# A hybrid decoder layer on one core: split token loads, reordered tile steps, new PSUM banks and filler around the FFN start

## The chip, the core and the metric

The program runs on one core of one Trainium2 chip. The core has five engines with a queue each: TensorE (PE, matmuls and transposes into PSUM; its weight loads are shown as PEld), VectorE (DVE), ScalarE (ACT), GpSimd (POOL) and SyncE (SP), which here only issues DMA. The metric is the device time of one execution in microseconds (us), the median over runs.

## What is computed

One inference step of one layer, for 1024 prompt tokens and 8 x 4 = 32 decode tokens (N = 1056 columns), d_model 1024, all in float32:

```
h = rms_norm(x, ln_mix_pre)
qa, ka, va, qkvb, bb, ab, zb, qc, gates = split(h @ w_in)
oa = sliding window attention with sinks (qa, ka, va)
ob = gated delta rule over chunks (qkvb, bb, ab), then norm and silu(zb)
oc = attention of qc over 256 memory tokens
up = einsum('blnc,ncd->blnd', stack(oa, ob, oc), w_branch)
mix = sum(sigmoid(gates) * up) @ w_out
x = x + rms_norm(mix, ln_mix_post)
gt, uf = split(rms_norm(x, ln_ffn_pre) @ w_ffn_in)
x = x + rms_norm((silu(gt) * uf) @ w_ffn_out, ln_ffn_post)
```

## The kernel before

**Number format.** Every float32 product of the large matrices is made of three matmuls: both operands are split into a high part (hi, rounded) and a low part (lo, the rest), and hi x hi, hi x lo and lo x hi are added in PSUM. So a weight panel, once it has landed in `raw`, is split on POOL in two steps (L839 and L842, or L900 and L902 in `split_to`) into `wsp` or, for the output projection, into `wo_top`, `wo_mk`, `wo_br`, `wo_ac` and, for the last one, a half of `wsp`. Activations are split on ACT (hi) and DVE (lo).

**Tiling.** The 1056 columns are three chunks of CH = 352. A chunk of a panel is 8 blocks x 3 passes = 24 matmuls of 128 x 352 and one PSUM bank. `raw` and `wsp` have two slots; panel n uses slot n % 2, and `load` waits for the split of n - 2.

**Stages**, in order of time:
- Opening (to 60 us). Eleven token tiles: 0 to 7 of the prompt, 8 the decode tokens, 9 and 10 the memory. For each: ACT squares it (L1579), DVE makes the mean (L2013), ACT the root (L1584), DVE the reciprocal (L2015) and scales into `xs` (L2017); PE transposes it (L958); ACT copies the hi part (L1588) and DVE the lo part (L2023) into `actT`. ACT and DVE run these in a software pipeline, `tile_a(t)`: squares and norm of tile t + 1, hi and lo of tile t - 1. PE puts the six chunks of the first two panels (L994) between transposes. SP loads x in `load_pair`, tiles 2 and 3, 4 and 5, 6 and 7, and weights between them.
- Input projection, 27 panels (L970), to 394 us.
- Middle stage: eight tiles of 128 tokens, each a list of steps TILE that all engines walk through. Each tile holds the delta rule (decay `dec` and `decm`, `at`, the inverse in `xt` and `xx`), six score groups ("S", transposed in "T", applied in "V") and 144 gate matmuls (L1152) as filler.
- Decode stage: the 32 decode tokens, with the last eight gate panels as filler (`gate_mm`, L1232), 576 matmuls in all.
- Branch stage (1086 to 1240 us). 12 panels, three branches of four (r = j // 4). For panel j SP loads weights (`load_wb`) and the stored gates (`load_q`, tile `gat`); ACT makes the sigmoid (L1921); PE does six half chunks of 12 matmuls (L1458) into banks 0 to 2; DVE multiplies them with the gate and adds to `accT` (L2443, or L2448 and L2450). Branch inputs come by `load_br(r)` into `brw` (2.1 MB) and are split by `hi_br` on ACT (L1910) and `lo_br` on DVE (L2418). The mixed sum `accT` is split in the same way, `lo_mix(m)` for m = 0 to 3 whole (L2424), for m = 4 to 7 by chunk.
- Output projection: nine blocks of token rows, `out_rows(t)` (L1481, 48 matmuls of 128 x 512), each normed, added to x, normed again and transposed back (`turn_back`, L1492).
- FFN: 22 steps of a loop of gate panel, up panel (L1466) and output panel (L1524).

**Order around the change.** Each engine works through its queue in the order of the code, and waits for semaphores. `x_here(n)` lets SP wait for token tile n. `x_lo`, `x_nm` count lo parts and scaled tiles, `w_lo` split panels, `g_mm` finished chunks of PE, `g_ev` evacuated banks, `b_hi` and `b_lo` split branch and mix parts, `q_sg` sigmoids, `q_mx` mixed chunks, `f_st` finished stores of the decode stage, `u_lo` row blocks that are back in `actD`, `t_y` normed row blocks. UO is the count of chunks at the end of the branch stage.

## Time and profile before

| what | value |
|---|---|
| median of 3 runs | 2156.93 us (2152.8 to 2168.03) |
| the profiled execution | 2157.78 us, its span 2156.0 us |
| PE busy | 2084.3 us, 97% |
| DVE / ACT / POOL busy | 46% / 24% / 35% |
| mean granted clock of PE | 0.986 |
| DMA | 193.80 MB, 90 GB/s over the span |
| chain that ended last | PE 85%, DVE 7%, ACT 4%, DMA 2%, issue 2% |

How to read it: the span is covered by PE nearly throughout, so the idle time of other engines costs nothing by itself; what counts is where PE stands still, and who releases it then. The granted clock is the share of full speed (2.4 GHz) that PE had; 0.50 is its lower level, 1.2 GHz.

### The profile page before, as it was taken

What the parts mean: (1) busy time and instruction counts of PE and PEld (TensorE: products, weight loads), DVE (VectorE), ACT (ScalarE), POOL (GpSimd) and SP (SyncE); (2) the same over time, 40 slices, a digit from 0 to 9 for tenths busy, and PEclk for the clock granted to TensorE, in tenths of its full rate; (3) what the DMA queues carried; (4) which work ended last, traced back from release to release, by engine and by line L of the source; (5) the groups of instructions that cost most, each with busy time, mean ns of one, the idle gap of its engine ahead of it and who ended that gap; (6) DMA issues with size and microseconds to landing.
All of it is one profiled execution on the core that took longest, in us unless ns stands there. A gap on an engine that the chain in (4) does not pass through costs nothing.

```text
span 2156.0 us, 34339 instructions
## 1 busy us (share of the span) xinstructions
PE 2084.3 (97%) x13511; PEld 2017.7 (94%) x13511; DVE 995.4 (46%) x1667; ACT 515.7 (24%) x1137; POOL 761.0 (35%) x325
## 2 busy tenths in 40 slices
PE   6999999999999999999999979999999999999998
PEld 5999999999999999999889968899999999999997
DVE  5754620355555555411347944533434353434435
ACT  5333621333333333321032222200000000000002
POOL 3334873111110111122136531343443434443444
PEclk8999999999999999999999999999999999999999
DMA  5223333433222332164375432111111111111114
GB/s 179 90 79 101 109 99 104 131 100 100 64 72 75 92 100 65 43 179 123 99 238 183 157 117 81 61 40 48 49 39 48 49 39 49 39 49 48 49 39 172
DMA packets 221271, 193.80 MB, mean 90 GB/s; under 512 B 24715, under 2 KB 192267, under 8 KB 221154
## 3 DMA queue, kind: packets, MB, share of 16 engines
q1 hardware_dynamic: 207042, 182.72, 27.5%
q10 hardware_dynamic: 14128, 9.65, 1.4%
q8 instruction: 73, 1.20, 0.2%
q14 instruction: 28, 0.23, 0.0%
HBM read 146.26 MB, written 47.09 MB: 90 GB/s over the span
## 4 chain that ended last, share of the span: by engine, by line
PE 85%; DVE 7%; ACT 4%; DMA 2%; issue 2%; SPq 0%; ACTq 0%; DVEq 0%
PE psum L1466 23%; PE psum L970 13%; PE psum L1524 11%; PE psum L1080 7%; PE psum L1152 6%; PE psum L1481 5%; PE psum L1232 4%; PE psum L1458 3%; PE psum L1201 2%; ACT pr L1795 1%; PE psum L1190 1%; DMA brw<-s_br 1%; PE psum L1035 1%; PE psum L1174 1%; PE psum L994 1%
## 5 line engine op out<-in xcount | busy, mean ns | idle before, releaser
L839 POOL TENSOR_TENSOR wsp<-raw,kc 128x1024 fp32r<-128x1024 f32 x116 | 277.6, 2393 | 1179.6 <-PE psum L1152 434.0
L1466 PE MATMUL psum<-actD,wsp 128*128 128x352 f32 x3168 | 517.2, 323 | 0.9 <-DVE actD L2482 0.9
L1466 PEld LDWEIGHTS psum<-actD,wsp 128*128 128x128 f32 x3168 | 511.3, 189 | 1.1 <-DVE actD L2482 1.1
L842 POOL TENSOR_TENSOR wsp<-raw,wsp 128x1024 fp32r<-128x1024 f32 x116 | 288.4, 2486 | 9.1
L970 PE MATMUL psum<-actT,wsp 128*128 128x352 f32 (+1 forms) x1728 | 282.5, 324 | 0.0
L970 PEld LDWEIGHTS psum<-actT,wsp 128*128 128x128 f32 (+1 forms) x1728 | 272.7, 185 | 5.4
L2535 DVE TENSOR_TENSOR accT<-accT,psum 128x352 f32<-128x352 f32 x504 | 241.7, 520 | 50.1 <-PE psum L1524 50.1
L1524 PE MATMUL psum<-fT,wsp 128*128 128x352 f32 x1512 | 249.8, 323 | 0.4 <-DVE accT L2535 0.4
L1524 PEld LDWEIGHTS psum<-fT,wsp 128*128 128x128 f32 x1512 | 244.0, 188 | 0.7 <-DVE accT L2535 0.7
L1152 PE MATMUL psum<-actT,wsp 128*128 128x352 f32 x1152 | 216.4, 333 | 0.0
L2518 DVE TENSOR_TENSOR fr<-psum,sg 128x352 f32<-128x352 f32 x66 | 34.6, 524 | 380.7 <-PE psum L1466 379.3
L1152 PEld LDWEIGHTS psum<-actT,wsp 128*128 128x128 f32 x1152 | 184.2, 188 | 0.8
L1458 PE MATMUL psum<-actD,wsp 128*128 128x352 f32 x864 | 144.7, 329 | 9.1 <-DVE prd L2448 4.6
L1458 PEld LDWEIGHTS psum<-actD,wsp 128*128 128x128 f32 x864 | 142.4, 193 | 11.4 <-DVE prd L2448 6.3
L1977 ACT ACTIVATE sg<-psum 128x352 f32<-128x352 f32 x66 | 30.5, 464 | 433.8 <-PE psum L1466 433.8
L1232 PE MATMUL psum<-actT,wsp 128*128 128x352 f32 x576 | 110.2, 344 | 0.0
L1232 PEld LDWEIGHTS psum<-actT,wsp 128*128 128x128 f32 x576 | 97.8, 200 | 4.8 <-issue 4.5
L1985 ACT ACTIVATE fT<-fr 128x352 fp32r<-128x352 f32 x66 | 32.9, 498 | 237.2 <-DVE fr L2518 237.2
L1795 ACT ACTIVATE pr<-psum,asm 128x256 f32<-128x256 f32 x96 | 44.6, 469 | 125.6 <-DVE asm L2228 73.1
L2140 DVE TENSOR_TENSOR kd<-psum,par 128x512 f32<-128x512 f32 x8 | 5.5, 691 | 119.6 <-PE psum L1089 119.6
L2055 DVE TENSOR_SCALAR y<-cv,scT 128x1024 f32<-128x1024 f32 (+1 forms) x24 | 32.3, 1385 | 58.3 <-ACT y L1655 54.5
L2058 DVE SCALAR_TENSOR_TENSOR y<-cv,scT,y 128x1024 f32<-128x1024 f32 x72 | 58.1, 854 | 0.9 <-DVE y L2058 0.4
(426 smaller groups left out, 2600.0 us busy)
## 6 DMA issues: line engine op xcount, KB each, us to landing
raw<-in_w_in SPq DMA_DIRECT2D x100, 256.0 KB, 4.0
raw<-in_w_ffn_in SPq DMA_DIRECT2D x88, 256.0 KB, 3.2
gat<-s_gate SPq DMA_DIRECT2D x12, 1056.0 KB, 5.3
raw<-in_w_ffn_out SPq DMA_DIRECT2D x44, 256.0 KB, 2.8
s_gate<-gst SPq DMA_DIRECT2D x48, 176.0 KB, 1.8
s_qkv<-y SPq DMA_DIRECT2D x12, 528.0 KB, 3.0
brw<-s_br SPq DMA_DIRECT2D x3, 2112.0 KB, 9.9
raw<-in_w_branch SPq DMA_DIRECT2D x24, 256.0 KB, 5.2
```

The lines of the kernel that those rows point to most:

```text
L839: pool.tensor_tensor(wsp[:, slot, 0], raw[:, slot], ones.unsqueeze(1).to_broadcast([P, KT, P]), ALU.mult).then_inc(w_hi, 1)
L842: pool.tensor_tensor(wsp[:, slot, 1], raw[:, slot], wsp[:, slot, 0].bitcast(F32), ALU.subtract).then_inc(w_lo, 1)
L970: mm = pe.matmul(psum[0:m, c, 0:CH], wsp[:, slot, a, k, 0:m], actT[:, h, k, CH * c:CH * c + CH], start=(k == 0 and q == 0), stop=(k == KT ...
L1080: mm = pe.matmul(psum[:, bank, w * h:w * h + w], lhs(h), rhs(h), start=True, stop=True)
L1152: mm = pe.matmul(psum[:, c, 0:CH], wsp[:, (NPB + j) % 2, a, kt, :], actT[:, h, kt, CH * c:CH * c + CH], start=(n % 24 == 0), stop=(n % 24 ...
L1232: mm = pe.matmul(psum[:, c, 0:CH], wsp[:, (NPB + m) % 2, a, k, :], actT[:, h, k, CH * c:CH * c + CH], start=(y % 24 == 0), stop=(y % 24 == ...
L1458: mm = pe.matmul(psum[:, c, 0:CH], slab(wsp[:, :, a], slot)[:, k, P * half:P * half + P], actD[:, h, a4 + k, CH * c:CH * c + CH], start=(k ...
L1466: mm = pe.matmul(psum[:, bank, 0:CH], wsp[:, slot, a, k, :], actD[:, h, k, CH * c:CH * c + CH], start=(k == 0 and q == 0), stop=(k == KT - ...
L1481: mm = pe.matmul(psum[0:rows, 2 * slot + half, :], actD[:, h, (k + 4) % 8, P * t:P * t + rows], wo_part(k, a)[:, 512 * half:512 * half + 512],
L1524: mm = pe.matmul(psum[:, 4 + x % 4, 0:CH], wsp[:, slot, a, m, :], fT[:, fs, h, CH * c:CH * c + CH], start=(q == 0), stop=(q == 2))
L1795: mm = act.activation(pr[:, a, :], psum[:, 3, 256 * a:256 * a + 256], ACT.Exp, scale=A_SC[j], bias=asm[:, S_NM, 2 * j + a:2 * j + a + 1], ...
L2535: dve.tensor_tensor(accT[:, m, cols], accT[:, m, cols], psum[:, 4 + x % 4, 0:CH], ALU.add).then_inc(o_ad, 1)
```

## The change

It has six parts.

1. **Opening.** Token tiles 2 and 3 are loaded one by one, each followed by a weight panel, and the pairs (4, 5) and (6, 7) wait for tiles 2 and 3. On DVE the mean of tile t + 1 stands ahead of the lo part of tile t - 1.
2. **Middle stage.** On DVE the multiplication `decm` moves from its own step to the head of step "KK", behind the score maximum and its two small steps of group 0.
3. **Decode stage.** The filler of gate matmuls is dealt out anew: 78 instead of 72 first, 18 instead of 12 ahead of the memory scores, 17 instead of 18 ahead of each of eight, 10 instead of 14 ahead of `update(7)`. The sum stays 576.
4. **Branch stage.** `load_br(1)` is issued ahead of the weights and gates of panel 2, `load_br(2)` at j == 3 instead of 4. The sigmoid of panel 2 stands ahead of the hi parts of branch 1. The hi and lo parts of mix 0 to 3 come half a panel to a panel sooner.
5. **Output projection.** The row blocks use banks 3 to 6 instead of 0 to 3 and the transposes back banks 0 and 1 instead of 4 and 5; PE's wait for g_ev ahead of them is gone; the split of the last projection weights on POOL also waits for the lo parts of the first chunk.
6. **FFN start.** Chunks 0 and 1 of the up panel (NPF + 1) are done between and behind the last two transposes back, ahead of chunk 2 of the gate panel, in banks 5 and 6. The third panel (NPF + 2) is split on POOL after five chunks instead of three, since it overwrites the gate panel.

```
-    X_LAND = ((0, 16), (1, 16), (0, 32), (0, 32), (1, 32), (1, 32), (0, 48), (0, 48), (1, 48), (0, 64), (0, 64))
+    X_LAND = ((0, 16), (1, 16), (0, 32), (1, 32), (0, 48), (0, 48), (1, 48), (1, 48), (0, 64), (1, 64), (1, 64))
...
         x_here(0)
-        load_pair(2)
+        sp.dma_start(xin[:, 2, :], x_view[2]).then_inc(x_in[0], 16)
         load_b(0)
         x_here(1)
-        load_pair(4)
+        sp.dma_start(xin[:, 3, :], x_view[3]).then_inc(x_in[1], 16)
         load_b(1)
         x_here(2)
+        load_pair(4)
+        x_here(3)
         load_pair(6)
...
         sp.wait_ge(f_st, F_ST)
+        load_br(1)
         for c in range(3):
             sp.wait_ge(gs_st[c], 16 + 16 * 24)
         for j in range(12):
             if j + 2 < 12:
                 load_seq(W_N["b", j + 1] - NPD + 1, W_N["b", j + 2] - NPD + 1)
                 load_q(j + 2)
-            if j in (0, 4):
-                load_br(j // 4 + 1)
+            if j == 3:
+                load_br(2)
...
                 if j == 7:
                     pool.wait_ge(g_mm, 6 + UO)
+                    pool.wait_ge(b_lo, 1 + MIX_N(0, 7) + 1)
...
-                    done = (3, 6, 9)[j]
+                    done = (5, 6, 9)[j]
...
-        gate_mm(72)
+        gate_mm(78)
         pe.wait_ge(f_in, F_IN)
...
-        gate_mm(12)
+        gate_mm(18)
         pe.wait_ge(f_dv, DVn("el"))
...
-            gate_mm(18)
+            gate_mm(17)
             mem_scores(b)
...
-        gate_mm(14)
+        gate_mm(10)
         update(7)
...
-                        mm = pe.matmul(psum[0:rows, 2 * slot + half, :], actD[:, h, (k + 4) % 8, P * t:P * t + rows],
+                        mm = pe.matmul(psum[0:rows, 3 + 2 * slot + half, :], actD[:, h, (k + 4) % 8, P * t:P * t + rows],
...
-
-        pe.wait_ge(g_ev, 3 + UO)
...
-                mm = pe.transpose(psum[:, 4 + k // 4, P * (k % 4):P * (k % 4) + rows],
+                mm = pe.transpose(psum[:, k // 4, P * (k % 4):P * (k % 4) + rows],
...
-            full_chunk(NPF % 2, c, 6 + c)
+            full_chunk(NPF % 2, c, (7, 2)[c])
         turn_back(NT - 1, 1, P)
+        pe.wait_ge(w_lo, NPF + 1 + 3)
+        pe.wait_ge(t_y, 2 + NT)
+        full_chunk((NPF + 1) % 2, 0, 5)
         turn_back(NT, 0, NS)
+        pe.wait_ge(u_lo, 2 + 6)
+        full_chunk((NPF + 1) % 2, 1, 6)
...
-        full_chunk(NPF % 2, 2)
-        in_panel(NPF + 1, (NPF + 1) % 2, g_ev, 3 + UF)
+        full_chunk(NPF % 2, 2, 3)
+        in_panel(NPF + 1, (NPF + 1) % 2, g_ev, 3 + UF, chunks=(2,))
...
+        def sigmoid(j):
+            act.wait_ge(q_in[j % 2], 16 * (j // 2) + 16)
+            act.activation(gat[:, j % 2], gat[:, j % 2], ACT.Sigmoid).then_inc(q_sg, 1)
+
         for j in range(12):
+            if j == 2:
+                sigmoid(j)
             for half in range(2):
                 if (j, half) in BR_AT:
                     hi_br(*BR_AT[j, half])
-            if j == 11:
-                for m in range(4):
+            if j >= 10:
+                for m in (2 * (j - 10), 2 * (j - 10) + 1):
...
+            if first:
+                mean(t + 1, 1 - b, first)
             if last:
                 lo_x(t - 1, 1 - b, last[0], last[1], last[2] if last[1] is memT else P * t - P)
...
-                elif step == "DEC":
+                elif step == "KK":
                     dve.wait_ge(dec_ok, 2 * t + 2)
                     dve.wait_ge(mrk_ok, t + 1)
                     dve.wait_ge(kq_ok, t + 1)
                     dve.tensor_tensor(decm[:], dec[:], mrk[:], ALU.mult).then_inc(dm_ok, 1)
-                elif step == "KK":
...
-                if j >= 10:
-                    lo_mix(2 * (j - 10) + half)
+                if 2 * j + half >= 19 and 2 * j + half < 23:
+                    lo_mix(2 * j + half - 19)
```

The rest of the diff gives ACT and DVE the new bank numbers.

What the change does to the order of instructions is shown at three places. First DVE, at the start of the first tile of the middle stage. L2147 (L2164 in the change) is `decm`; `asm` holds the score maximum and what follows from it. Before:

```order
118 L2140 TENSOR_TENSOR kd<-psum,par 128x512
119 L2142 TENSOR_TENSOR vb<-psum,par 128x512
120 L2147 TENSOR_TENSOR decm<-dec,mrk 128x512
121 L2220 TENSOR_REDUCE asm<-psum 128x2
122 L2223 SCALAR_TENSOR_TENSOR asm<-asm,snk 128x2
123 L2226 TENSOR_TENSOR asm<-asm,snk 128x2
124 L2152 TENSOR_TENSOR at<-psum,decm 128x512
```

With the change:

```order
118 L2157 TENSOR_TENSOR kd<-psum,par 128x512
119 L2159 TENSOR_TENSOR vb<-psum,par 128x512
120 L2236 TENSOR_REDUCE asm<-psum 128x2
121 L2239 SCALAR_TENSOR_TENSOR asm<-asm,snk 128x2
122 L2242 TENSOR_TENSOR asm<-asm,snk 128x2
123 L2164 TENSOR_TENSOR decm<-dec,mrk 128x512
124 L2168 TENSOR_TENSOR at<-psum,decm 128x512
```

`decm` has moved behind the three steps of the scores, next to `at`, which reads it; the same holds in all eight tiles.

Second SP's queue at the start of the branch stage; `s_br` is the stored branch input, `s_gate` the stored gates. Before:

```order
236 L723 DMA s_br<-dob 128x4x32
237 L649 DMA raw<-in_w_branch 64x4x256 x2
238 L672 DMA gat<-s_gate 128x2x1056
239 L667 DMA brw<-s_br 128x4x1056
240 L649 DMA raw<-in_w_branch 64x4x256 x2
241 L672 DMA gat<-s_gate 128x2x1056
```

With the change:

```order
236 L725 DMA s_br<-dob 128x4x32
237 L669 DMA brw<-s_br 128x4x1056
238 L651 DMA raw<-in_w_branch 64x4x256 x2
239 L674 DMA gat<-s_gate 128x2x1056
240 L651 DMA raw<-in_w_branch 64x4x256 x2
241 L674 DMA gat<-s_gate 128x2x1056
```

The load of `brw` has moved ahead of the weights (row 238) and the gates (row 239) of panel 2.

Third PE around the last two transposes back (L1492, L1494 in the change); L1466 (L1470) are the chunks of the first FFN panels. Before:

```order
827 L1492 MATMUL psum<-kc,xs 128x128 x8
828 L1466 MATMUL psum<-actD,wsp 128x352 x48
829 L1492 MATMUL psum<-kc,xs 128x128 x8
830 L1492 MATMUL psum<-kc,xs 128x32 x8
831 L1466 MATMUL psum<-actD,wsp 128x352 x120
```

With the change:

```order
827 L1494 MATMUL psum<-kc,xs 128x128 x8
828 L1470 MATMUL psum<-actD,wsp 128x352 x48
829 L1494 MATMUL psum<-kc,xs 128x128 x8
830 L1470 MATMUL psum<-actD,wsp 128x352 x24
831 L1494 MATMUL psum<-kc,xs 128x32 x8
832 L1470 MATMUL psum<-actD,wsp 128x352 x96
```

One chunk of 24 matmuls now stands between the two transposes; the number of chunks is the same.

## Rows read from the trace of the kernel before

**Rows 1.** TensorE's waits over the whole span: total us, times, longest

```profile
PE psum L958 <- DVE xs L2017: 20.1, 6, 9.2
...
PE psum L1190 <- ACT pr L1795: 12.5, 16, 1.5
...
PE psum L1458 <- DVE prd L2448: 4.6, 5, 2.9
...
PE psum L1247 <- DMA da<-s_qc: 2.0, 1, 2.0
...
PE psum L1291 <- DVE del_ L2302: 1.6, 1, 1.6
```

**Rows 2.** Chain of work (start, us), then a window (busy, granted clock, DMA share)

```profile
1429.72 19.24 PE psum L1466 x120
...
1250.00:1254.00 4.00, 2.83 (x7) 2.25 (x8) 3.38 (x8) 1.13 (x3) 0.00 (x0) 0.50 0.19 76
```

**Rows 3.** Timeline of the opening: start us, us, engine, line [idle before <-releaser]

```profile
8.19 1.06 ACT L1579 ACTIVATE xjunk<-xin 128x1024 f32<-128x1024 f32 x1 [0.61 <-DMA xin<-in_x_prompt]
...
12.09 0.78 SPq L477 DMA_DIRECT2D xin<-in_x_prompt  x1
...
19.44 3.42 DVE L2017 SCALAR_TENSOR_TENSOR xs<-xin,rs,gbc 128x1024 f32<-128x1024 f32 x1
...
27.84 5.04 PE L994 MATMUL psum<-actT,wsp 128*128 128x352 f32 x24
...
28.02 1.28 DVE L2017 SCALAR_TENSOR_TENSOR xs<-xin,rs,gbc 128x1024 f32<-128x1024 f32 x1
...
31.53 1.28 DVE L2017 SCALAR_TENSOR_TENSOR xs<-xin,rs,gbc 128x1024 f32<-128x1024 f32 x1
...
45.35 1.09 PE L958 MATMUL psum<-kc,xs 128*128 128x128 f32 x8 [1.53 <-DVE xs L2017]
```

**Rows 4.** Timeline of the first steps of tile 1 of the middle stage

```profile
460.64 2.38 POOL L842 TENSOR_TENSOR wsp<-raw,wsp 128x1024 fp32r<-128x1024 f32 x1
...
461.74 1.82 DVE L2147 TENSOR_TENSOR decm<-dec,mrk 128x512 f32<-128x512 f32 x1 [1.93 <-ACT dec L1769]
...
463.49 0.68 DVE L2220 TENSOR_REDUCE asm<-psum 128x2 f32<-128x512 f32 x1
...
464.50 0.69 DVE L2152 TENSOR_TENSOR at<-psum,decm 128x512 f32<-128x512 f32 x1
...
465.47 0.66 PE L1190 MATMUL psum<-kc,pr 128*128 128x128 f32 x4 [1.54 <-ACT pr L1795]
```

**Rows 5.** DMA issues of 1100.27, 1100.69 and 1101.20 (KB each, us to landing)

```profile
gat<-s_gate SPq DMA_DIRECT2D x1, 1056.0 KB, 7.2
...
brw<-s_br SPq DMA_DIRECT2D x1, 2112.0 KB, 14.1
...
raw<-in_w_branch SPq DMA_DIRECT2D x2, 256.0 KB, 13.8
```

**Rows 6.** Timeline at panel 2 of the branch stage

```profile
1116.78 1.95 ACT L1921 ACTIVATE gat<-gat 128x2112 f32<-128x2112 f32 x1
...
1120.98 48.01 PE L1458 MATMUL psum<-actD,wsp 128*128 128x352 f32 x288 [3.97 <-DVEq L2445]
```

**Rows 7.** Timeline between branch stage and output projection

```profile
1240.13 7.82 DVE L2424 TENSOR_TENSOR actD<-accT,actD 128x352 fp32r<-128x352 f32 x4
...
1244.63 2.50 POOL L902 TENSOR_TENSOR wsp<-raw,wsp 128x1024 fp32r<-128x1024 f32 x1
...
1248.86 1.82 DVE L2424 TENSOR_TENSOR actD<-accT,actD 128x352 fp32r<-128x352 f32 x4
...
1251.17 4.93 PE L1481 MATMUL psum<-wo_top,actD 128*128 128x512 f32 x12 [10.92 <-DVE prd L2448]
```

**Rows 8.** Timeline of TensorE at the start of the FFN

```profile
1371.45 1.03 PE L1492 MATMUL psum<-kc,xs 32*128 32x32 f32 x8 [3.19 <-DVE actD L2482]
...
1373.41 40.88 PE L1466 MATMUL psum<-actD,wsp 128*128 128x352 f32 x240 [0.93 <-DVE actD L2482]
```

More of the change, by code:

```diff
@@ L1985, in hi_f @@
                 act.activation(fT[:, fs, 0, CH * c:CH * c + CH], fr[:, CH * c:CH * c + CH], ACT.Copy).then_inc(f_hi, 1)
-        gt_panel(0, 0, banks=(6, 7, 2))
+        gt_panel(0, 0, banks=(7, 2, 3), order=(1, 2, 5))
         hi_f(0, 0)
@@ L1997, in _ @@
             act.wait_ge(t_tr, 9 + t + 1)
[L1998 removed]
+            act.activation(jk[0:rows, :], rows_psum(2 * slot, rows), ACT.Square,
                            accum_out=ns[0:rows, slot % 2, slot // 2, 0:1]).then_inc(t_sq, 1)
@@ L2008, in _, with mean, norm @@
         dve.wait_ge(k_in, 16 * 2)
-        def norm(n, slot, rows, gain):
+        def mean(n, slot, rows):
             dve.wait_ge(x_sq, n + 1)
             dve.tensor_scalar(rs[0:rows, slot, 1:2], rs[0:rows, slot, 0:1], 1.0 / D, EPS, ALU.mult, ALU.add).then_inc(x_rs, 1)
+        def norm(n, slot, rows, gain):
             dve.wait_ge(x_rt, n + 1)
@@ L2239, in dve_tile @@
                         level(2)
-                elif step[0] == "D":
+                elif step[0] == "D" and step != "DEC":
                     f = step[1]
@@ L2508, in _, with mul_f @@
         dve.memset(accT[:], 0.0).then_inc(o_ad, 1)
-        def mul_f(i):
-            for c in range(3):
+        def mul_f(i, banks=(0, 1, 2)):
+            for c, bank in enumerate(banks):
                 cols = slice(CH * c, CH * c + CH)
@@ L2542, in step_f @@
             add_out(i - 1, range(4, KT))
-        mul_f(0)
+        mul_f(0, banks=(5, 6, 2))
         lo_f(0, 0)
```

33 lines of the change are left out of this document (16 added, 17 removed).

## The prediction

> **What bounds the kernel.** The profile's first part comes first: TensorE (PE) is busy for 97% of the span, so only three things can shorten the run: PE's idle time, PE's time at half clock, and less work on it. The diff removes no matmul. So the next view is PE's waits: 20.1 + 12.5 + 4.6 + 2.0 + 1.6 [rows 1], and in the timelines 4.0 [rows 6], 10.9 [rows 7] and 3.2 + 0.9 [rows 8], 59.8 us together. A warm chunk (24 matmuls) takes 19.24 / 5 = 3.85 us, a matmul 0.16 [rows 2]. The window at the end of the wait of 10.9 has a granted clock of 0.50 [rows 2]: PE works at 1.2 instead of 2.4 GHz, so a removed wait returns the slow time behind it too. The sum is made against the profiled execution, 2157.8 us (span 2156.0 and 1.8 around it); the median of the runs shown, 2156.9, needs no correction.
>
> **Opening.** PE's first chunk follows the transposes of tile 4 and starts at 27.84; ahead of it DVE scales a tile every 3.51 us (L2017 at 28.02 and 31.53) [rows 3]. In this cycle stand mean, ACT's root and reciprocal between the low part and the scaling. With the mean ahead, mean and root run under the low part: some 0.5 less a tile. The pair of tiles 2 and 3 held the queue from tile 1's landing at 8.19 to 12.09 [rows 3], so tile 2 alone lands 2.0 earlier. Part of this is eaten again: tiles 4 and 5 are asked for only then, behind three transfers, and POOL's weight splits still hold one scaling (L2017 took 3.42 instead of 1.28) [rows 3]. I take 3.1 for the first chunk and 1.4 of the wait of 1.53 for tile 9 [rows 3]: **4.5**, bounds 2.5 (only the shorter cycle, 5 x 0.5) and 6.5 (2.0 for the load, 2.5 for the cycle, 2.1 for the hold).
>
> **Tiles.** In each of the eight tiles of the middle stage DVE now takes the score maximum (L2220) ahead of decm (L2147). PE waits for the exponentials that follow, 1.54 in this tile [rows 4]; of 12.5 us in 16 waits [rows 1] seven are of this kind. The maximum could start 3 us before 463.49: decm began at 461.74, when ACT had the decay, and took 1.82 us where such an operation takes 0.69 (L2152), ending 0.54 after POOL's split step (460.64 to 463.02) [rows 4]. So POOL holds a DVE operation with two SBUF operands. The maximum reads PSUM and passes, but its next step (L2223: asm and snk, both SBUF) is held to 463.02; before, it came at 463.49 + 0.71 = 464.20. That is 1.2. `at` follows decm, which ends some 0.4 later than 463.56; but `at` stood behind the maximum before, so it starts at 464.1 instead of 464.50, and with PE 1.2 ahead the inverse's transposes may wait 0.2. Seven by 1.0: **7.0**, bounds 3 (the inverse waits 0.8) and 10.8 (7 x 1.54, no hold).
>
> The Trainium skill (SBUF — State Buffer, Who interferes with whom) calls this an exclusive lock: a DVE instruction with two SBUF inputs and a GpSimd instruction that reads SBUF block each other fully, and a tensor_reduce is never held. By it a tile gains 1.2, without it 1.54; the trace's 1.82 agrees with the lock.
>
> **Decode stage.** Six gate matmuls more stand ahead of the wait for f_in (2.0) and six ahead of that for `el` (1.6) [rows 1]; each six fills 6 x 0.16 = 0.96. They come from fillers ahead of eight score steps (one each) and of an update (four), where PE has no wait now: **1.9**, bounds 0 (it waits there instead) and 2.5 (with clock).
>
> **Branch stage, panel 2.** Its gates were issued at 1100.27 and landed 7.2 later, at 1107.5 [rows 5], but their sigmoid began at 1116.78 [rows 6]: two ACT copies of brw stood ahead, and brw landed at 1100.69 + 14.1 = 1114.8 [rows 5]. PE waited 4.0 [rows 6] and, by the clock of rows 2, some 3.4 us of half clock cost 1.7 more. Now the sigmoid goes first. The load also goes 2.4 earlier, ahead of panel 2's weights, and transfers land in order of issue: weights behind brw took 13.8 [rows 5]. brw's 2.1 MB needed 7.3 (1107.5 to 1114.8), so it lands near 1106, the weights near 1108.5, and their split, two POOL steps of 2.4 [rows 4], ends at 1113.3. PE wants them at 1120.98 - 4.0 - 5.8 (three chunks of 12 matmuls into free banks) = 1111.2 [rows 6]. A new wait of 2.1 takes the place of 5.7: **3.6**, bounds 1.5 and 5.7.
>
> The Trainium skill (DMA: Bandwidth & Descriptors, Queues, rings and completion order) says that each DMA engine takes descriptors in ring order, which speaks against this early load: by it the term is 3.6, by free sharing of the queue up to 5.7. The 13.8 agrees with the order.
>
> **Panel 6** is the same once more: the load moves one panel ahead; 2.9 of the waits for prd [rows 1] is here, with 1.7 of slow clock. DVE has little slack after it: **3.5**, bounds 1 and 5.
>
> **Ahead of the output projection** PE stops for 10.92 us [rows 7]. It waited for the last evacuation, which stood in DVE's queue behind four low parts (L2424). These took 7.82 instead of 1.82 (the same four at 1248.86) while POOL split the last projection weights [rows 7]. That wait of PE is gone, since the rows use banks 3 to 6, and this split waits for the low parts. Low parts 0 to 3 come half a panel sooner, so the first row block can run k = 0 to 3 at once: 24 matmuls of 0.16 x 512 / 352 = 0.23, 5.6 us, while the others need 1.8. The split then runs from about 1240.5 to 1245.4 and is wanted at k = 7, 42 x 0.23 = 9.8 after 1240.25. Behind it on POOL wait the first FFN split and the residual adds; the first add is wanted only by a transposition two row blocks (22 us) later. The slow start, 4.93 instead of 12 x 0.23 = 2.8 [rows 7], goes too: **13.0**, bounds 10 and 13.5.
>
> **FFN start.** PE waits 3.19 and 0.93, and its next chunk takes 40.88 - 9 x 3.85 = 6.2 instead of 3.85 [rows 8, 2]: 6.4 us. Two chunks of the second panel now fill this. But the third panel's weights may be split only after five chunks instead of three, and the split (4.8) has one chunk (3.85) as cover: 1.0 of new wait. **5.4**, bounds 4 and 6.4.
>
> Sum: 4.5 + 7.0 + 1.9 + 3.6 + 3.5 + 13.0 + 5.4 = 38.9; 2157.8 - 38.9 = **2118.9 us**. The lower bounds add up to 22.0 (2135.8), the upper ones to 50.4 (2107.4).
>
> **Rivals.**
> - The stop moves into the output projection: low parts 4 to 7 are held by POOL's earlier splits (7.8 instead of 1.8), or the norm gains and residual rows, which SP can send only when DVE has finished, come late. For it: DVE is a chunk behind when PE ends. Against: 5.6 us of ready work. It costs 7.8 - 5.6 = 2.2 with slow clock behind it and, in the row loads, up to 5: 2125. Chance 0.12.
> - The early 2.1 MB loads starve weights and gates, so both branch terms vanish. For it: 13.8 behind brw. Against: the second load has a whole panel of slack. 2118.9 + 7.1 = 2126. Chance 0.12.
> - The tile reorder does not do what it says, because POOL holds the maximum's next step as long as the old order did; 7.0 becomes 1, 2125. It needs a hold to 464.2, past the step's end at 463.02. Chance 0.08.
> - Slower: decm now stands behind three steps that need scores, so behind awin and qz from DMA. If those are late, the decay chain at, xt, inverse stalls in all eight tiles. It decides once that chain is (38.9 - 7.0) / 8 = 4.0 us a tile later than PE can use it; at 7 us the time is 2157.8 - 31.9 + 56 = 2182. Against: the loads are issued a tile ahead, and PE's waits have no row for them. Chance 0.03.
> - As summed, 2110 to 2130: 0.60. The last 0.05 is several of these at once, up to no change.
>
> **The numbers.** A measurement here tells 1%, 21.6 us, from no change. The forecast and its first three rivals each pass that; the mixed case (0.05) and a share of 0.03 of the rivals with low bounds elsewhere do not. So faster 0.89, same 0.08, slower 0.03. The range runs from the upper bounds, 2107, to just past the lower ones, 2137.
>
> **What would show it.** First L994 chunk at 24 to 25 us; waits of PE for pr of a few tenths; panel 2's sigmoid at the landing of its gates, with a wait of PE of about 2 for weights; no wait and a granted clock of 1.0 between the last branch chunk and the first projection rows; 1 us of wait for the third FFN split. The forecast is wrong if PE stops within the projection rows, if L1190 waits as before, or if a step of the FFN loop changes, which the sum takes as untouched.

## The result and the profile after

| what | before | after |
|---|---|---|
| median | 2158.8 us (4 runs) | 2123.9 us (4 runs: 2119.8 to 2134.7) |
| ratio after / before | | 0.9836, 95% interval 0.9804 to 0.9868 |
| profiled execution; span | 2157.8; 2156.0 us | 2124.25; 2122.4 us |
| PE busy; granted clock | 97%; 0.986 | 98%; 0.993 |

The change makes the kernel 1.6% faster; the interval of the ratio lies wholly below 1, from 1.3 to 2.0%. It is 34.9 us between the medians and 33.6 between the spans; forecast were 38.9. The profile after, first PE's waits over the whole span (total us, times, longest):

```profile
PE psum L962 <- DVE xs L2032: 16.1, 5, 9.2
PE psum L1462 <- DVE prd L2464: 5.8, 3, 2.9
PE psum L1194 <- ACT pr L1802: 2.9, 15, 0.2
PE psum L1462 <- DVE actD L2416: 1.8, 1, 1.8
PE psum L1251 <- DMA da<-s_qc: 1.2, 1, 1.2
...
PE psum L1295 <- DVE del_ L2318: 0.6, 1, 0.6
PE psum L1470 <- POOL wsp L845: 0.3, 1, 0.3
```

The waits for `pr` fell from 12.5 to 2.9, those of 10.9 ahead of the output projection and 3.2 at the FFN start are gone [rows 1, 7, 8]. But in the branch stage (L1462, L1458 before) PE still waits 5.8 + 1.8 us, in part at places where it hardly waited before. The timeline of PE through this stage and into the projection rows (L1485) shows where (start us, us, engine, line, [idle before <- releaser]):

```profile
1070.76 3.96 PE L1462 MATMUL psum<-actD,wsp 128*128 128x352 f32 x15
1076.52 22.51 PE L1462 MATMUL psum<-actD,wsp 128*128 128x352 f32 x129 [1.79 <-DVE actD L2416]
1099.18 52.40 PE L1462 MATMUL psum<-actD,wsp 128*128 128x352 f32 x324 [0.15 <-POOL wsp L905]
1153.98 13.54 PE L1462 MATMUL psum<-actD,wsp 128*128 128x352 f32 x72 [2.41 <-DVE prd L2464]
1168.00 34.90 PE L1462 MATMUL psum<-actD,wsp 128*128 128x352 f32 x216 [0.47 <-DVE prd L2464]
1205.83 19.14 PE L1462 MATMUL psum<-actD,wsp 128*128 128x352 f32 x108 [2.94 <-DVE prd L2464]
1224.81 2.95 PE L1485 MATMUL psum<-wo_top,actD 128*128 128x512 f32 x12
```

A panel is 72 matmuls. So PE stops in panel 0 (1.79; before, 0.53), not at panel 2 (0.15 instead of 3.97), in panel 6 (2.41, as before), and in panel 10 (2.94; before, waits of 0.2 to 0.4). The stage took 153.8 us, before 153.5: it gained nothing. This is no accident of the two executions: from its first to its last matmul it took 153.5 to 156.1 us in the profiles of the four kernels with the old branch stage (before and, in the experiments, b_tiles, b_mean and b_load), and 153.8, 153.7 and 156.7 in the three with the new one (after, a_gev, a_nopw).

The time between the first matmuls of two stages, in both profiled executions, tells what each part brought:

| stretch | before | after | gain | forecast |
|---|---|---|---|---|
| opening, to the first matmul of the third panel | 59.7 | 56.5 | 3.2 | 4.5 |
| input projection | 338.5 | 337.0 | 1.5 | 0 |
| middle stage (tiles) | 513.2 | 504.5 | 8.7 | 7.0 |
| decode stage | 175.0 | 172.8 | 2.2 | 1.9 |
| branch stage, first to last matmul | 153.5 | 153.8 | -0.3 | 7.1 |
| gap ahead of the projection + projection | 11.3 + 108.2 | 0.2 + 106.3 | 13.0 | 13.0 |
| FFN start, to the first output panel | 54.7 | 49.4 | 5.3 | 5.4 |
| the rest | 741.9 | 741.9 | 0 | 0 |

So the sum's error of 5.3 us is the branch stage's 7.4, in part covered by other terms; 1.5 of this cover, the input projection, is luck.

### The profile page after: what moved, and what is told of

It is laid out like the page before. It is cut to its first block, busy times and chain, and to the rows that moved or that the text cites. A ratio compares the mean times of both kernels' runs of the same rounds, so it can differ in the third digit from the quotient of the medians.

```text
span 2122.4 us, 34341 instructions
## 1 busy us (share of the span) xinstructions
PE 2081.3 (98%) x13511; PEld 2014.4 (95%) x13511; DVE 1003.6 (47%) x1667; ACT 515.5 (24%) x1137; POOL 758.0 (36%) x325
## 4 chain that ended last, share of the span: by engine, by line
PE 89%; DVE 5%; DMA 2%; ACT 1%; issue 1%; SPq 1%; POOL 0%; DVEq 0%; POOLq 0%; ACTq 0%
PE psum L1470 24%; PE psum L974 13%; PE psum L1531 11%; PE psum L1084 7%; PE psum L1156 6%; PE psum L1485 5%; PE psum L1462 4%; PE psum L1236 4%; PE psum L1205 2%; PE psum L1178 1%; PE psum L998 1%; PE psum L1194 1%; ACT pr L1802 1%; PE psum L1039 1%; PE psum L1573 1%
## 5 line engine op out<-in xcount | busy, mean ns | idle before, releaser
L1470 PE MATMUL psum<-actD,wsp 128*128 128x352 f32 x3168 | 515.8, 323 | 1.0 <-ACT sg L1990 0.6
L1470 PEld LDWEIGHTS psum<-actD,wsp 128*128 128x128 f32 x3168 | 509.1, 188 | 1.6 <-issue 0.9
L1462 PE MATMUL psum<-actD,wsp 128*128 128x352 f32 x864 | 146.4, 332 | 7.8 <-DVE prd L2464 5.8
L1462 PEld LDWEIGHTS psum<-actD,wsp 128*128 128x128 f32 x864 | 144.2, 195 | 10.0 <-DVE prd L2464 7.1
```

Of the source, the lines that this page charges most:

```text
L1462: mm = pe.matmul(psum[:, c, 0:CH], slab(wsp[:, :, a], slot)[:, k, P * half:P * half + P], actD[:, h, a4 + k, CH * c:CH * c + CH], start=(k ...
L1470: mm = pe.matmul(psum[:, bank, 0:CH], wsp[:, slot, a, k, :], actD[:, h, k, CH * c:CH * c + CH], start=(k == 0 and q == 0), stop=(k == KT - ...
```

## Experiments

Each kernel is compared with the kernel before on the same chip; stretches are read from its profiled execution. "Panels 0 to 2, 3 to 8, 9 to 11" are PE's waits in these parts of the branch stage; where two numbers stand, the first is panel 0 and the second the stop in panel 2.

| kernel | ratio, 95% interval | panels 0-2 | 3-8 | 9-11 |
|---|---|---|---|---|
| before | 1 | 0.53 + 3.97 | 3.75 | 0.84 |
| after | 0.9836 (0.9804 to 0.9868) | 1.79 + 0.15 | 2.88 | 2.94 |
| a_nopw | 0.9845 (0.9803 to 0.9887) | 0.67 + 3.70 | 3.58 | 4.13 |
| a_brold | 0.9871 (0.9834 to 0.9907) | 0.63 + 2.63 | 3.87 | 3.28 |
| a_br2mid | 0.9818 (0.9779 to 0.9856) | 0 | 1.19 | 4.14 |
| a_lo | 0.9813 (0.9782 to 0.9845) | 0 | 3.61 | 3.14 |
| a_p1 | 0.9822 (0.9791 to 0.9853) | 2.76 + 1.78 | 2.89 | 2.96 |
| a_gev | one execution | 0.66 + 3.00 | 3.62 | 3.28 |
| a_o3 | 0.9828 (0.9781 to 0.9876) | 0.62 + 4.28 | 3.80 | 3.11 |
| a_both | 0.9852 (0.9811 to 0.9893) | 3.07 + 1.97 | 1.68 | 3.05 |
| a_w2 | 0.9816 (0.9783 to 0.9849) | 3.12 + 0 | 1.19 | 3.62 |

### The opening: each half alone

Edits to the kernel before, each with one execution (2169.07 and 2157.93 us; the kernel before beside them had a median of 2162.1, from 2152.0 to 2169.1), so that only the trace tells something. First the loads (with the loads of tiles 3 to 7 and the landing counts as in the change):

```
-        load_pair(2)
+        sp.dma_start(xin[:, 2, :], x_view[2]).then_inc(x_in[0], 16)
...
```

> The kernel before with one part of the opening alone: tiles 2 and 3 loaded one by one, mean where it was. In the changed kernel the first full chunk began 2.25 us sooner (25.59 for 27.84), where 3.1 had been forecast. Theory 'landings': what comes first is set by when tiles 2, 4 and 5 land, and the load split gives nearly all: first chunk 1.5 to 2.3 us sooner than in the kernel before (25.5 to 26.3). Theory 'cycle' (the forecast's: 0.5 us a tile from the mean): the load gives at most 0.5 at the first chunk (27.3 or later), since DVE's cycle of 3.5 us a tile and POOL's hold eat it. In both, DVE scales a tile every 3.5 us in the steady part.

And the mean:

```
+            if first:
+                mean(t + 1, 1 - b, first)
             if last:
                 lo_x(t - 1, ...
```

> The kernel before with the other part of the opening alone: mean of the next tile ahead of the low part, loads as they were. Theory 'landings': first chunk at most 1.0 us sooner (26.8 or later), the steady cycle 3.15 us instead of 3.51, as in the changed kernel, so the gain comes only over the tiles behind the fifth. Theory 'cycle': first chunk 1.5 to 2.5 us sooner (25.3 to 26.3), 0.5 us a tile.

Timeline of b_load, then of b_mean: the first full chunk.

```profile
21.71 3.27 DVE L2019 SCALAR_TENSOR_TENSOR xs<-xin,rs,gbc 128x1024 f32<-128x1024 f32 x1
...
26.65 5.79 PE L996 MATMUL psum<-actT,wsp 128*128 128x352 f32 x24
```

```profile
22.07 2.00 DVE L2019 SCALAR_TENSOR_TENSOR xs<-xin,rs,gbc 128x1024 f32<-128x1024 f32 x1
...
25.75 5.99 PE L994 MATMUL psum<-actT,wsp 128*128 128x352 f32 x24
```

The loads alone gave 1.2 us at the first chunk and 0.4 at the end of the opening; the mean alone 2.1 and 2.8; both 2.2 and 3.2 in the changed kernel's profile. So "landings" falls, although the loads' 1.2 lies between what the two theories gave them. The second half of "cycle" holds in its size (the mean carries most), its 0.5 us a tile does not: DVE's steady cycle went from 3.51 us to 3.15 in the changed kernel and 3.31 in b_mean. The two kernels also differ in how long POOL held DVE's scaling just before the first chunk (the rows above, 3.27 against 2.00 us), so up to 1.3 us of the difference between them may be this hold and not the edits. This hold is not the same in every execution. In two kernels whose opening is the same, first a_gev:

```profile
21.27 1.28 DVE L2034 SCALAR_TENSOR_TENSOR xs<-xin,rs,gbc 128x1024 f32<-128x1024 f32 x1
21.46 3.33 POOL L845 TENSOR_TENSOR wsp<-raw,wsp 128x1024 fp32r<-128x1024 f32 x1
```

then a_nopw:

```profile
20.83 2.34 POOL L845 TENSOR_TENSOR wsp<-raw,wsp 128x1024 fp32r<-128x1024 f32 x1
20.90 3.35 DVE L2031 SCALAR_TENSOR_TENSOR xs<-xin,rs,gbc 128x1024 f32<-128x1024 f32 x1
```

Who comes first, by 0.07 or 0.19 us, takes its normal time and the other gets 1.0 to 2.1 us longer. Of the ten executions with this opening (after and nine kernels below) four (a_p1, a_lo, a_br2mid, a_gev) never had a scaling held to over 3 us like this, and their first chunk began at 23.3 to 24.2; the six others began at 25.5 to 26.1. The opening ended 4.6 to 6.5 us sooner than before in the four and 2.5 to 3.7 in the six. The Trainium skill (SBUF — State Buffer, SBUF: two separate sides) says that whichever of the two starts first gets the port pair for its whole instruction; the rows agree.

### The tiles alone

On the kernel before, the three lines of `decm` moved from step "DEC" to the head of step "KK".

> The kernel before with the reordered DVE steps of the middle stage's tiles alone. In the changed kernel this stage was 8.7 us shorter. Theory: the order does all of it: the stage shorter by 8 to 9.5 us, PE's waits for the exponentials 0.2 each, ratio 0.9955 to 0.9965. Rival: part of the 8.7 comes from the different phase in which the stage is entered (loads and POOL's splits stand otherwise against PE after the opening's 4.7): then 5 to 7 us here, ratio 0.997 to 0.998. Second rival (from the forecast): what the stage gains, the decode stage behind it loses, because the branch input it must load stays where it was: then total below 5 us.

Ratio 0.9953, interval 0.9932 to 0.9973; the middle stage is 8.7 us shorter, and PE's waits for `pr` fell as in the changed kernel. This stretch was 8.5 to 8.8 us shorter in every kernel with the new order. The first theory holds: the order does all of it, independent of the phase in which the stage is entered. Tile 1 in the profile after:

```profile
454.97 0.69 DVE L2236 TENSOR_REDUCE asm<-psum 128x2 f32<-128x512 f32 x1 [0.45 <-PE psum L1178]
455.35 2.38 POOL L845 TENSOR_TENSOR wsp<-raw,wsp 128x1024 fp32r<-128x1024 f32 x1
455.69 2.05 DVE L2239 SCALAR_TENSOR_TENSOR asm<-asm,snk 128x2 f32<-128x2 f32 x1
457.89 0.69 DVE L2164 TENSOR_TENSOR decm<-dec,mrk 128x512 f32<-128x512 f32 x1
...
458.86 0.66 PE L1194 MATMUL psum<-kc,pr 128*128 128x128 f32 x4 [0.21 <-ACT pr L1802]
```

The maximum passes beside POOL, its next step, on two columns only, is held to 457.74, the end of POOL's step (455.35 + 2.38 = 457.73), and still PE waits 0.21 instead of 1.54 [rows 4]. In the rows 4 `decm` was itself held to 1.82; now it takes 0.69, since the hold has been served by the small step.

### The output projection

Two single edits of the changed kernel. One takes POOL's new wait away, one puts PE's old wait back.

```
-                    pool.wait_ge(b_lo, 1 + MIX_N(0, 7) + 1)
```

> The changed kernel without POOL's new wait for the low parts of the first chunk ahead of the split of the last projection weights. Theory 'banks' (the rows' own banks 3 to 6 carry the gain at the output projection): POOL may start this split when the last branch matmul ends, at 1224.6, and in the changed kernel it started at 1225.34, so only 0.7 us is at stake: first projection rows begin at once after the last branch matmul as before, span within 1 us of the changed kernel, ratio to the kernel before 0.983 to 0.985. Theory 'POOL hold' (the forecast's: the split would hold low parts 4 to 7, 7.8 us instead of 1.8): PE stops 2 to 5 us in the projection rows, ratio 0.985 to 0.9875.

```
+        pe.wait_ge(g_ev, 3 + UO)
```

> The changed kernel with PE's old wait ahead of the projection rows put back: it waits for the last evacuation of the branch stage although its rows now have their own banks. Theory 'banks' (what is worth 11.1 us between the last branch matmul and the rows, and 1.9 behind it, is that PE no longer waits here): in the changed kernel DVE ended that evacuation near 1232.0, 7.4 us behind the last branch matmul, so PE waits 7 to 8 here, plus 1 to 2 of half clock behind it: gap plus projection 8 to 10 us longer than in the changed kernel. Theory 'POOL hold gone' (POOL's later split alone had already made the evacuations quick): wait below 3.

Without POOL's wait: gap and projection 13.0 us shorter than before, as with it. With PE's wait (timeline of PE in a_gev):

```profile
1219.39 2.19 PE L1462 MATMUL psum<-actD,wsp 128*128 128x352 f32 x12 [0.48 <-DVE prd L2466]
1229.42 5.49 PE L1485 MATMUL psum<-wo_top,actD 128*128 128x512 f32 x12 [7.84 <-DVE prd L2466]
```

It waits 7.84, the next 12 matmuls take 5.49 instead of 2.95, and gap and projection are 10.5 us longer than in the changed kernel. So the banks carry 10.5 of the 13.0; the other 2.5, by which this kernel is still shorter than the kernel before, is not taken apart by any run. The wait on POOL is worth nothing: in the profile after, POOL's split began 0.37 us behind the end of the last branch matmul (1205.83 + 19.14 = 1224.97), in a_nopw 0.08. There it holds the first chunk's four low parts (3.52 us), in the changed kernel, with the wait, the second chunk's:

```profile
1225.34 1.89 POOL L903 TENSOR_TENSOR wsp<-raw,kc 128x1024 fp32r<-128x1024 f32 x1 [4.25 <-PE psum L1462]
...
1227.54 4.03 DVE L2440 TENSOR_TENSOR actD<-accT,actD 128x352 fp32r<-128x352 f32 x4
```

### The branch stage, undone and shifted

a_brold: both loads of `brw` and the sigmoid as in the kernel before.

```
-        load_br(1)
...
-            if j == 3:
-                load_br(2)
+            if j in (0, 4):
+                load_br(j // 4 + 1)
...
-            if j == 2:
-                sigmoid(j)
...
```

> The changed kernel with the branch part undone: both later loads of brw and the sigmoid's place as in the kernel before. The forecast gave this part 3.6 (panel 2) + 3.5 (panel 6); the profiles of before and after give 5.2 and 0.7. Theory 'by term': PE's wait at panel 2 comes back (3 to 4.5 us, for the sigmoid), panel 6 keeps a wait of 2 to 3 of about the size the changed kernel has (2.41), and the branch stage is 3 to 6 us longer than the changed kernel's 153.8 (some 158), ratio to the kernel before 0.985 to 0.9875. Rival 'no net gain': the wait for POOL's split of panel 2's weights, which a second execution of this order shows at 3.70 us, costs as much as the wait for the gates did: branch stage within 1.5 us of the changed kernel's, ratio 0.983 to 0.985.

PE waited 2.63 for the gates at panel 2, 2.99 and 0.88 for `prd` in panels 6 and 7. The branch stage took 157.3 us, 3.5 more than in the changed kernel: "by term" is what the waits at panel 2 and 6 say. But it is only 0.6 more than in a_nopw (156.7), whose branch loads are the new ones and whose PE waited 3.70 us for the split weights at panel 2, as the rival has it. The ratios' intervals overlap too. What the branch part is worth as a whole is not shown; it lies within what executions differ by.

a_br2mid: only the second load moves, behind the weights of panel 6.

```
+                if j == 4:
+                    load_br(2)
                 load_q(j + 2)
-            if j == 3:
-                load_br(2)
```

> The changed kernel with the second of the two early loads put one weight pair later: brw for panels 8 to 11 is asked for after the weights of panel 6 instead of ahead of the second output-projection weights, still ahead of the gates of panel 6. Theory 'pile-up' (the wait of 2.41 at panel 6 stays because the projection weights land late behind brw, at 1136.1, and four pairs of POOL's splits then run back to back from 1136.1 to 1155.7 and hold each of DVE's additions): here POOL's splits start near 1131 with pauses between them, the additions in panel 5 are held half as often, and PE's wait in panel 6 falls to 0 to 1.2. Rival 'low parts': DVE is late there because four low parts of 1.25 to 3 us stand in two panels, wherever POOL's splits are: the wait stays at 2 to 3. Rival 'landing': brw now lands late and its copies hold the gates' sigmoid: wait of 1.5 to 4 for ACT or gates. Ratio to the kernel before 0.982 to 0.984 by the first, 0.983 to 0.986 by the others.

POOL in panels 5 and 6, first in the profile after:

```profile
1136.14 1.89 POOL L903 TENSOR_TENSOR wo_top<-raw,kc 128x1024 fp32r<-128x1024 f32 x1 [8.86 <-DMA raw<-in_w_out]
1138.11 2.57 POOL L905 TENSOR_TENSOR wo_top<-raw,wo_top 128x1024 fp32r<-128x1024 f32 x1
1140.63 2.18 POOL L903 TENSOR_TENSOR wsp<-raw,kc 128x1024 fp32r<-128x1024 f32 x1
...
1152.46 3.28 POOL L905 TENSOR_TENSOR wsp<-raw,wsp 128x1024 fp32r<-128x1024 f32 x1
```

and DVE beside it, an addition with both operands in SBUF that takes 0.53 when POOL rests:

```profile
1134.67 0.53 DVE L2466 TENSOR_TENSOR accT<-accT,prd 128x352 f32<-128x352 f32 x1
...
1138.88 2.18 DVE L2466 TENSOR_TENSOR accT<-accT,prd 128x352 f32<-128x352 f32 x1
```

In a_br2mid the same splits start at 1128.39 and pause after the second pair:

```profile
1128.39 2.02 POOL L903 TENSOR_TENSOR wo_top<-raw,kc 128x1024 fp32r<-128x1024 f32 x1 [2.11 <-DMA raw<-in_w_out]
...
1142.27 1.90 POOL L903 TENSOR_TENSOR wo_mk<-raw,kc 128x1024 fp32r<-128x1024 f32 x1 [4.44 <-DMA raw<-in_w_out]
```

and PE runs from panel 0 into panel 6 without a stop (480 matmuls):

```profile
1073.94 78.80 PE L1462 MATMUL psum<-actD,wsp 128*128 128x352 f32 x480
1153.16 9.89 PE L1462 MATMUL psum<-actD,wsp 128*128 128x352 f32 x60 [0.43 <-DVE prd L2464]
```

PE's waits in panel 6 were together 2.41 to 2.85 us in all six executions with this load as in the changed kernel (after, a_nopw, a_lo, a_p1, a_gev, a_o3), the longest 2.40 to 2.43, and 0.43, 0.67 and 0.42 in the three with it moved (a_br2mid, a_both, a_w2). "Pile-up" is shown. The branch stage took 147.6 us in a_br2mid, 6.2 less than in the changed kernel; 1.7 of this is less waiting in panels 3 to 8, most of the rest comes from panels 0 to 2, which ran without a stop (see "How much is chance").

a_lo: low and high parts 0 to 3 of the sum back at their old places.

> The changed kernel with the low parts 0 to 3 of the branch sum (and ACT's high parts) put back to their old places, half a panel later. In the changed kernel PE waits 2.94 at 1205.83, in panel 10, where the kernel before waited 0.2 to 0.4. Theory 'moved low parts': the wait comes from the low parts, now in panels 9 and 10 between two back-to-back splits of POOL: here the waits of panels 9 to 11 are together below 1.2, the branch stage 2.5 to 5 us shorter, and the output projection is at most 1 us longer, because the first row block needs low part 3 only 7.4 us after it starts; ratio 0.9815 to 0.9835. Rival 'POOL alone': DVE's additions are held by the splits there wherever the low parts stand, waits of 2 to 4 remain in panels 9 to 11, and the ratio is that of the changed kernel, 0.9836. Rival 'the stop moves': PE waits 2 to 5 in the first row block for low part 3 or 4.

PE waits 3.14 in panel 10, no less than in the changed kernel (2.94). So the moved low parts are not needed for it. In this kernel POOL splits four pairs from 1190.20 to 1209.1 without a pause; in the changed kernel it pauses 1.9 us between the second and third of them, and a low part of 3.42 stands behind. The kernels of the opening bear this out. b_load has the whole old branch stage, low parts included, and in it POOL splits the four pairs from 1213.59 to 1232.49 without a pause. PE then waits as in a_lo (rows of POOL, DVE and PE):

```profile
1222.88 2.19 POOL L902 TENSOR_TENSOR wo_br<-raw,kc 128x1024 fp32r<-128x1024 f32 x1
...
1230.19 3.42 DVE L2426 TENSOR_TENSOR actD<-accT,actD 128x1056 fp32r<-128x1056 f32 x1
...
1234.10 19.11 PE L1460 MATMUL psum<-actD,wsp 128*128 128x352 f32 x108 [2.79 <-DVE prd L2450]
```

In before, b_mean and b_tiles, with the low parts at the old place and a pause of 2.1 to 2.2 us between the second pair and the third, the waits of panels 9 to 11 are 0.8 to 0.9 together. In after and a_brold, with a pause of 1.9 to 2.0 and the low parts moved, they are 2.94 and 3.28. By these seven executions either is enough, splits without a pause or the moved low parts: DVE has no reserve there. No run changes the pause alone.

a_o3: the fourth pair of projection weights ahead of panel 9's.

```
-             ("b", 8), ("b", 9), ("o", 3), ("b", 10)
+             ("b", 8), ("o", 3), ("b", 9), ("b", 10)
```

> The changed kernel with one entry of the order of weights moved: the fourth pair of output-projection weights is loaded and split ahead of the branch weights of panel 9 instead of behind them. In panels 9 and 10 of the changed kernel POOL splits four pairs (4 x 4.6 = 18.5 us in 21.1) and PE waits 2.94 there; it waited 3.14 with the low parts at their old place, 3.28 with the old loads. Theory 'POOL share': with three pairs there and the fourth in panel 8, where POOL stood idle 7.7 us, DVE catches up: waits in panels 9 to 11 together 0 to 1.3, branch stage 2.5 to 5 us shorter than in the changed kernel; ratio to the kernel before 0.981 to 0.983. Rival 'DVE alone': DVE has 6.6 us of evacuations and a low part or two in each 11.5, so the wait only moves to panel 8 or stays: waits of 2 to 4 in panels 7 to 11, ratio 0.983 to 0.985.

The wait moved from panel 10 to panel 11 (2.66 at 1212.77) and kept its size. "POOL share" falls, the rival stands: what is late next takes the place.

### The entry of the branch stage

a_p1: POOL splits panel 1's weights only behind the second chunk's low parts.

```
+                if j == 1:
+                    pool.wait_ge(b_lo, 1 + 8)
```

> The changed kernel with one wait more on POOL: the split of the weights of panel 1 begins only when DVE has the second chunk's four low parts. In the changed kernel this split (1071.6 to 1076.1) held those four to 5.18 us instead of 1.83, and PE waited 1.79 for them, with half the clock around it. Theory 'hold': the low parts take 1.8, PE's wait at the second chunk is 0 to 0.3, the split ends by 1079 and panel 1 begins without a wait; branch stage 2 to 4 us shorter than the changed kernel's 153.8, ratio 0.982 to 0.9835. Rival: PE is simply early and the stop moves to panel 2 (wait for the split of its weights, 2 to 4), which is set by the loads behind the last decode store and not by PE: branch stage as before, ratio 0.9836.

In the profile after POOL's split holds these four low parts to 5.18 (the first four took 1.83):

```profile
1071.58 1.89 POOL L903 TENSOR_TENSOR wsp<-raw,kc 128x1024 fp32r<-128x1024 f32 x1 [6.40 <-DMA raw<-in_w_branch]
...
1072.15 5.18 DVE L2416 TENSOR_TENSOR actD<-brw,actD 128x352 fp32r<-128x352 f32 x4 [0.63 <-ACT actD L1911]
```

In a_p1 these four are free of the hold, and the third chunk's four get it:

```profile
1072.46 1.83 DVE L2418 TENSOR_TENSOR actD<-brw,actD 128x352 fp32r<-128x352 f32 x4 [0.60 <-ACT actD L1913]
1074.42 1.90 POOL L903 TENSOR_TENSOR wsp<-raw,kc 128x1024 fp32r<-128x1024 f32 x1 [6.32 <-DVE actD L2418]
1074.93 5.24 DVE L2418 TENSOR_TENSOR actD<-brw,actD 128x352 fp32r<-128x352 f32 x4 [0.44 <-ACT actD L1913]
```

PE waited 0.97 and 1.79 for low parts in panel 0 and 1.78 at panel 2. So the cause is right (1.83 for 5.18), but the stop only moved on, and the stage was 1.4 us longer than in the changed kernel: as a remedy the theory falls, to the rival's side.

a_both (a_br2mid and a_o3 together) and a_w2 (a_br2mid, and panel 2's weights asked for ahead of the stores):

> The changed kernel with both: brw's second load behind the weights of panel 6, and the fourth projection weights ahead of panel 9's. Theory: the two remedies add, since they act on panels 5 and 6 and on 9 and 10: from panel 3 to the last branch matmul PE waits less than 1.5 us together (5.8 in the changed kernel, 4.9 with the load alone), the branch stage is 147 to 149 us long, and the ratio to the kernel before is 0.978 to 0.9815, below the changed kernel's 0.9836. Rival: the chip's clock in the decode stage, which made that stage 8 to 11 us longer in three of nine executions, and the waits for brw and panel 2's weights, which come when PE is early, take it back: ratio 0.981 to 0.984.

```
         store_dec(1, "o_z")
+        load_wb(2)
         sp.wait_ge(g_ad, 8)
...
```

> The changed kernel with two edits of the load order: panel 2's branch weights asked for behind the second decode store, ahead of the eight stores of the recurrent state (issued over 11.2 us there) and of the wait for all decode stores; and brw's second load behind the weights of panel 6, which took PE's wait in panel 6 from 2.4 to 0.43 and 0.23. Theory 'late weights': the wait for POOL's split of panel 2's weights (3.70, 3.00, 4.28, 1.97, 1.78 and 0.15 in six executions with the early load of brw) comes from asking for them 13 to 14 us after the branch stage starts, behind stores and behind 2.1 MB of brw; here they land before the stage starts, their split follows panel 0, PE does not wait for POOL in panel 2, and panels 2 to 6 run with less than 1 us of waits: branch stage 148 to 151 us, ratio to the kernel before 0.978 to 0.982. Rival 'gates': panel 2's gates still land late (1099.7 in the changed kernel), so PE waits 2 to 4 for the sigmoid or the evacuation instead, ratio 0.982 to 0.985. Second rival: the earlier split holds the third chunk's low parts and PE waits 2 to 3 more in panel 0.

In a_both panel 6 waits only 0.67, panel 11 2.62 and panels 0 to 2 5.04. The branch stage took 153.8 us, and the ratio, 0.9852, is a little above even the rival's range: the two remedies do not add. In a_w2 PE runs from panel 0 to panel 6:

```profile
1076.27 0.75 PE L1464 MATMUL psum<-actD,wsp 128*128 128x352 f32 x3 [1.27 <-DVE actD L2418]
1078.87 75.80 PE L1464 MATMUL psum<-actD,wsp 128*128 128x352 f32 x459 [1.85 <-DVE actD L2418]
1155.08 9.87 PE L1464 MATMUL psum<-actD,wsp 128*128 128x352 f32 x60 [0.42 <-DVE prd L2466]
```

So "late weights" is shown for panel 2: asked for at 1067.9 instead of 1084.5, their split began at 1089.0 and nobody waited for it, nor for the gates. The stage took 150.1 us, 3.7 less than in the changed kernel. But 3.1 us of waits in panel 0 (the second rival's 2 to 3, about what a_p1 and a_both had without this edit) and 3.1 in panel 10 are there, and the ratio, 0.9816, can't be told from the changed kernel's 0.9836. No kernel here beats it by more than a measurement tells.

### How much is chance

The changed kernel and the nine a_ kernels have the same decode stage. Two windows of its end, first of a_nopw, then of the changed kernel (columns: window, length, busy us of PE, PEld, DVE, ACT, POOL, granted clock, DMA share, GB/s):

```profile
1040.00:1080.00 40.00, 40.00 (x164) 30.60 (x163) 11.59 (x20) 3.56 (x9) 4.25 (x2) 0.71 0.44 131
```

```profile
1040.00:1070.00 30.00, 30.00 (x158) 23.17 (x157) 10.34 (x17) 2.08 (x6) 4.25 (x2) 0.94 0.58 174
```

From the same group of matmuls on (1041.55 and 1040.18) to the start of the branch stage (1080.26 and 1070.76) the first took 38.7 us and the second 30.6, so 8.1 longer; its clock was 0.50 from 1040 to 1055. Against the kernel before, the decode stage came out between 5.7 us shorter (a_gev) and 8.6 longer (a_lo) in these ten executions. That is most of the spread between the profiled executions, and it changes the branch stage too. In a_lo and a_br2mid the clock was 0.50 in the last part of the decode stage, after SP had asked for `brw`: PE's first branch matmul came 9.2 and 6.9 us behind ACT's first copy of `brw`, in the eight others 1.6 to 3.6. In these two the low parts and panel 2's weights were ready, panels 0 to 2 had no wait, and the stage took 147.5 and 147.6 us. What PE loses ahead of the stage it gets back in part within it.

## The prediction, point by point

**Opening, 4.5 forecast, 3.2 measured.** Failed was the split of the term: the load was taken to bring 2.0 earlier landing, the mean 0.5 a tile. The load alone brought 0.4, the mean 2.8 (one execution each). The forecast had the hold of one scaling by POOL stay; in four of ten executions it went, with 2 us more. Over these ten the opening gained 2.5 to 6.5 us, 4.1 on average, so that the size forecast is not refuted. Its upper bound adds up to 6.6, not 6.5. The further 1.5 of the input projection is no part of the change: PE, never idle there, ran a few us at half clock in the execution of before (72 matmuls in 13.36 us, which take 11.79 elsewhere). The same dip (13.35 to 13.37 us for 72 matmuls) stood in this stage in eight of the fourteen executions, in a_both twice, and nowhere in after. All nine dips stand right behind one of the eight groups of 18 matmuls with a single column (L980, 1.99 us), but 103 other such groups have none behind them; what sets it off stays open.

**Tiles, 7.0 forecast, 8.7.** The mechanism is right, and b_tiles shows it alone. Its price was too low: I let `decm` end 0.4 later and took 0.2 off for the inverse. But `decm` is no longer held and PE's wait goes from 1.54 to 0.21, 1.3 a tile in seven tiles, 9.3 at most.

**Decode stage, 1.9 forecast.** The two waits fell from 2.0 and 1.6 to 1.2 and 0.6, so 1.8. The stretch itself (2.2) can't show it, since it varies by 14 us over ten executions with the same decode stage.

**Panel 2, 3.6 forecast.** The sigmoid began at the landing of its gates, with the copies of `brw` behind, as forecast, and the new wait for the split weights, 2.1 by the forecast, came as 1.78 to 4.28 in five of eight executions with this order of loads. Two, entered late against `brw`, had none, and after had 0.15: because of the 1.79 and some clock lost in panel 0, PE reached panel 2 28.3 us after its first branch matmul, where a_nopw, a_gev and a_o3, with 0.6 to 0.7 lost, reached it after 25.6 to 25.9; the split was also ready a little sooner, after 28.4 us instead of 28.8 to 29.8. The forecast looked at panel 2 alone; the step that failed is that PE would arrive there as it did before. It enters the stage 3 us sooner against the first `brw`, which moved only 12.6 us (copied from 1069.16 instead of 1081.80) where PE moved 15.7 (1070.76 instead of 1086.44): it was asked for 14.8 us sooner, but landed 10.4 us after its issue instead of 8.2. A gain upstream meets a chain of loads that doesn't move with it.

**Panel 6, 3.5 forecast, 0.7.** Wait and slow clock went from 2.87 + 1.83 to 2.41 + 2.00, and the next wait from 0.88 to 0.47. The failed step is that moving the load one panel ahead removes 3.5 of the wait for `prd`: the wait was put down to `brw` landing late, but the 2.1 MB then delayed the projection weights queued behind them (asked for at 1124.0, landed at 1136.1), four pairs of splits ran back to back, and DVE, held, was as late as before. The Trainium skill's ring order (DMA: Bandwidth & Descriptors, Queues, rings and completion order), weighed for panel 2, bears on this too: by it the descriptors of the weights are taken behind those of `brw` on each DMA engine, and the trace agrees, with `brw` landed at 1133.3 and the weights 2.9 us later. Moved behind the weights, the load took most of the wait: 0.42 to 0.67 in the panel.

**Panels 9 to 11, no term.** Waits went from 0.84 to 2.94, with 1.8 of slow clock (108 matmuls in 19.14, at 0.16 each 17.3). The failed step is a term put at nothing without a reason: the low parts of the sum come sooner into panels where POOL splits for 19.1 of 21 us (1183.2 to 1204.2), though the prediction priced just such a hold ahead of the output projection (7.82 for 1.82) [rows 7]. But the moved low parts are not the only way to this wait: with them at the old place it was 2.79 in b_load and 3.14 in a_lo, where the splits ran without a pause. So part of it is how the loads happen to fall against PE.

**Ahead of the output projection, 13.0 and 13.0.** Right in size and cause: it came out at 13.0 to 13.1 us in eight of the nine executions without PE's old wait, and at 12.0 in a_lo, whose low parts come later. The part given to POOL's wait is nothing. Low parts 4 to 7 did not stop PE, so this rival fell.

**FFN start, 5.4 forecast, 5.3.** The new wait for the third split was 0.3 instead of 1.0, and one of 0.65 for ACT came, which the sum had not, so that some of the agreement is luck:

```profile
1352.93 4.10 PE L1470 MATMUL psum<-actD,wsp 128*128 128x352 f32 x24 [0.65 <-ACT sg L1990]
1357.34 23.36 PE L1470 MATMUL psum<-actD,wsp 128*128 128x352 f32 x144 [0.30 <-POOL wsp L845]
```

**Rivals.** The time alone, 2124.25, can't choose: it lies in the outcome "as summed" (2110 to 2130, chance 0.60) and beside three rivals (2125, 2126, 2125). That the total came so near is partly luck, since the branch stage gave nothing of its 7.1. By what happened in the stages the second rival (both branch terms vanish, 2126) is nearest. It had 0.12. Its reason, loads that starve others, holds for panel 6; at panel 2 the term came in this execution, and was lost in panels 0 and 10. The rivals on the tiles and on `decm` fell: that stage gained more than forecast. Of the signs named, PE did not stop in the projection rows, the waits for `pr` were 0.2, and no part of the FFN loop changed (741.9 us in both); the first chunk came at 25.6 instead of 24 to 25.

## What to carry to other kernels

Where one engine (here DVE) is nearly full and is held by another (here POOL), a wait removed in one panel can come back in a later one: price the engine over the whole stage, not the stop. A large load moved ahead must be followed to what is asked for behind it in the same queue, and from there to what that sets off together. Banks of its own for the next stage's output, by contrast, gave PE 10.5 us in the one kernel that undoes them, and with the rest of that part the forecast 13.0 in eight executions of nine, since they take PE off DVE's pace instead of quickening DVE.
